# A transformer stack with routed experts on one core: the experts' entry ordered by token tile, and weight splits moved around the last branch

## The reference, cut to what matters

```python
# merged = sum over branches of sigmoid(gate) * (branch @ w_br)
x = x + merged @ w_o                       # [256, 1024] @ [1024, 1024]
h = rmsnorm_2(x, g_ffn)
g_logits = h @ w_rg + b_rg                 # 4 groups
p_g = softmax(g_logits); g_sel = argmax(g_logits)
e_in = (h @ w_re + b_re) of the chosen group         # 8 experts
top_v, top_i = top_k(e_in, 2)
w2 = softmax(top_v) * p_g[g_sel]
for n in range(32):                        # expert n: group n // 8
    a, b = split(h @ w_up[n])              # [1024, 512]
    out += combine[:, n] * ((silu(a) * b) @ w_down[n])   # [256, 1024]
x = x + out
```

## Time and profile before

| | |
|---|---|
| median of 3 runs | 1603.18 us |
| profiled execution | 1604.8 us, of which the span from first to last instruction is 1603.0 us |
| PE busy | 1554.6 us, 97% of the span |
| DVE busy | 1241.9 us, 77% |
| ACT busy | 865.4 us, 54% |
| mean granted TensorE clock | 0.993 of full |
| chain that ended last | PE 87%, DVE 7%, ACT 4%, DMA 1% |

### The profile page before, as it was taken

The page is one execution under the profiler, slowest core; times in us unless marked ns, Lnnn a source line. Parts: engine busy times, 40 slices in busy tenths (PEclk is TensorE's granted clock), DMA queues, the critical chain, the costliest instruction groups (busy, mean ns, idle before and its releaser), DMA issues.

```text
span 1603.0 us, 19574 instructions
## 1 busy us (share of the span) xinstructions
PE 1554.6 (97%) x7617; PEld 1264.4 (79%) x7617; DVE 1241.9 (77%) x1864; ACT 865.4 (54%) x1264; POOL 66.2 (4%) x102
## 2 busy tenths in 40 slices
PE   7999999999999999999999999999999999999997
PEld 4888886888887888868888888777788877777875
DVE  2898877988869888673596655769878779898996
ACT  3535445544345443457454544555566458686874
POOL 1110100000001000000001000000001000000000
PEclk9999999999999999999999999999999999999999
DMA  9999855988857988323376554445324459898993
GB/s 345 375 379 347 290 193 192 336 300 300 296 184 253 311 299 289 127 77 106 106 257 193 169 165 158 133 150 192 106 80 128 158 185 361 319 345 300 368 343 115
DMA packets 196339, 373.78 MB, mean 233 GB/s; under 512 B 8986, under 2 KB 102608, under 8 KB 196240
## 3 DMA queue, kind: packets, MB, share of 16 engines
q1 hardware_dynamic: 176976, 301.60, 55.2%
q0 software_dynamic: 18864, 69.76, 12.9%
q10 hardware_dynamic: 400, 1.10, 0.2%
HBM read 371.38 MB, written 1.05 MB: 232 GB/s over the span
## 4 chain that ended last, share of the span: by engine, by line
PE 87%; DVE 7%; ACT 4%; DMA 1%; issue 1%; SPq 0%; DVEq 0%; ACTq 0%
PE banks L521 24%; PE banks L523 24%; PE banks L522 24%; DVE ul L458 1%; PE banks L1571 1%; PE banks L1544 1%; PE banks L1052 1%; PE banks L632 1%; PE banks L2657 1%; ACT uh L447 1%; PE banks L2101 1%; PE banks L1558 1%; DMA raw<-in_ffn_w_in 1%; DVE full L986 1%; PE banks L585 1%
## 5 line engine op out<-in xcount | busy, mean ns | idle before, releaser
L447 ACT ACTIVATE uh<-raw 128x1024 fp32r<-128x1024 f32 (+2 forms) x548 | 570.1, 1049 | 415.1 <-PE banks L523 411.6
L458 DVE TENSOR_TENSOR ul<-raw,uh 128x1024 fp32r<-128x1024 f32 (+2 forms) x548 | 658.4, 1210 | 167.8 <-ACT uh L447 159.9
L521 PE MATMUL banks<-uh,hh 128*128 128x512 f32 (+2 forms) x1296 | 516.1, 398 | 9.8 <-DVE hl L992 6.1
L523 PE MATMUL banks<-uh,hl 128*128 128x512 f32 (+2 forms) x1296 | 503.7, 389 | 0.0
L522 PE MATMUL banks<-ul,hh 128*128 128x512 f32 (+2 forms) x1296 | 502.7, 388 | 0.0
L521 PEld LDWEIGHTS banks<-uh,hh 128*128 128x128 f32 x1296 | 244.8, 189 | 65.4 <-DVE hl L992 9.5
L523 PEld LDWEIGHTS banks<-uh,hl 128*128 128x128 f32 x1296 | 244.1, 188 | 50.6
L522 PEld LDWEIGHTS banks<-ul,hh 128*128 128x128 f32 x1296 | 245.1, 189 | 46.1 <-issue 0.5
L521 PE MATMUL banks<-uh,bh 128*128 128x512 f32 x512 | 207.5, 405 | 2.0 <-DVE bl L2830 1.8
L523 PE MATMUL banks<-uh,bl 128*128 128x512 f32 x512 | 200.1, 391 | 0.0
L522 PE MATMUL banks<-ul,bh 128*128 128x512 f32 x512 | 199.7, 390 | 0.0
(11 more groups left out here) (350 smaller groups left out, 1292.3 us busy)
## 6 DMA issues: line engine op xcount, KB each, us to landing
raw<-in_ffn_w_in SPq DMA_DIRECT2D x176, 512.0 KB, 6.5
raw<-in_w_up SPq DMA_DIRECT2D x64, 1024.0 KB, 6.4
arena<-in_ada_w POOLq DMA_DIRECT2D x60, 1024.0 KB, 6.0
raw<-in_ffn_w_out SPq DMA_DIRECT2D x44, 1024.0 KB, 5.6
raw<-in_w_down SPq DMA_DIRECT2D x32, 1024.0 KB, 6.1
raw<-in_w_in SPq DMA_DIRECT2D x22, 1024.0 KB, 5.1
raw<-in_ada_w SPq DMA_DIRECT2D x12, 1024.0 KB, 10.8
raw<-in_w_mem_kv SPq DMA_DIRECT2D x4, 1024.0 KB, 5.3
```

The lines of the kernel that those rows point to most:

```text
L447: act.e.activation(uh[r][:, 0:w], raw[m % NRAW][:, h * w:(h + 1) * w], AF.Copy).then_inc(act_done, ta.put("hi", u))
L458: dve.e.tensor_tensor(ul[r][:, 0:w], raw[m % NRAW][:, h * w:(h + 1) * w], uh[r][:, 0:w].bitcast(F32), ALU.subtract).then_inc(dve_done, tv. ...
L521: pe.e.matmul(o, a, wh, start=k + j == s0, stop=False)
L523: mm = pe.e.matmul(o, b, wh, start=False, stop=k + j == s1)
```

## The change

Five things change, all from the last branch on.

1. **Splits around the last branch.** ACT splits the last two `w_br` units of branch 1 ahead of the sigmoids of that branch (before, behind them). DVE splits one unit of `wo` ahead of its merge of c=0, and the second behind it (before, both ahead).
2. **wo by tile at its end, and the entry by tile.** The last two of the 8 `wo` units are first used for tile 0, then for tile 1. The first tile's addition to `x`, its transposes and its router product start while PE still multiplies tile 1. All three `keep_busy` blocks are changed: 10, 10 and 10 become 0, 5 and 3. ACT loads the table of the square root before the sums of squares. DVE's scaled copies of `x` (`normed`, `gx`) move behind the group's choice, and the gather takes all of tile 0 before tile 1, so that the second copy is due only halfway.
3. **Second selection.** `sel` of group 1 and the two MAX instructions are made before the gathered tokens are split, and side work no longer makes it.
4. **First experts.** ACT computes the second weight (Exp) and loads the Silu table between its splits, and the number of units that ACT and DVE split ahead in the experts 0 to 3 is capped until the middle of the expert (`FIRST_HIGH`, `FIRST_LOW`). The next group's side work starts at expert 4 of a group instead of 2.
5. **The end.** The last `md` is computed by column half, so the first half's split may start while PE is at the second. The stores of tile 1 are issued by ACT, those of tile 0 by SP.

```diff
-        def units_dve(dve, key, K, mid=None, mid_k=None):
-            k = 0
+        def units_dve(dve, key, K, mid=None, mid_k=None, ahead=None):
+            k, cap = 0, len(units) if ahead is None else dve.unit_at + ahead
             while k < K:
-                split_low(dve, dve.unit_at + NUNIT - 1)
+                split_low(dve, min(cap, dve.unit_at + NUNIT - 1))
                 u, kk, n = take_unit(dve, key)
                 if mid is not None and k >= (K // 2 if mid_k is None else mid_k):
                     mid()
-                    mid = None
-                split_low(dve, u + NUNIT - 1)
+                    mid, cap = None, len(units)
+                split_low(dve, min(cap, u + NUNIT - 1))
...
+            got = [take_unit(pe, ("wo",)) for _ in range(2)]
+            for t in range(T):
+                for i, (u, kk, n) in enumerate(got):
+                    if (t, i) == (1, 1):
+                        hf_turn_pe(pe, 0)
+                    mm = tile_products(pe, u, kk, n, KD - 2 + i, t, lh, ll, parts_ready(pe, "ga"), WO_BANKS[t], -1,
+                                       KD - 1)
...
+            split_high(act, act.unit_at + 3)
             sigmoid_act(act, 1)
             held_act(act, ("br",), 4, 2)
...
-            held_dve(dve, ("br",), 4, 2)
+            held_dve(dve, ("br",), 4, 1)
             merge_dve(dve, 1, 0)
+            split_low(dve, dve.unit_at + 1)
             plain_dve(dve, "ga", KD, hh, hl, bk=GA_BANKS, groups=(0, 1))
...
         def route_pe(pe):
-            keep_busy(pe, 7, 10)
...
-            keep_busy(pe, 0, 10)
+            keep_busy(pe, 0, 5)
...
-            keep_busy(pe, 0, 10)
-            gather_pe(pe, 0, 0, 4)
-            gather_pe(pe, 0, 1, 5)
+            keep_busy(pe, 0, 3)
+
+            pe.wait_ge(dve_done, tv("sel", 0, 1))
+            for t in range(T):
+                pe.wait_ge(dve_done, tv("gx", t))
+                for q in range(2):
...
         def route_act(act):
+            act.e.activation(st[:, 258:259], sum4[:, 0:1], AF.Sqrt).then_inc(act_done, ta.put())
...
+        def second_weight_act(act):
+
+            yield from idle(0.3)
+            yield 0.3
             act.wait_ge(dve_done, tv("dv"))
             act.e.activation(ez, dv, AF.Exp).then_inc(act_done, ta.put("ez"))
+            silu_table_act(act)
...
+        FIRST_HIGH, FIRST_LOW = {0: 7, 1: 4, 2: 4, 3: 4}, {0: 5, 1: 3, 2: 3, 3: 3}
...
+            def last_outp():
+
+                got = [take_unit(pe, ("md", 31)) for _ in range(2)]
+                for c in range(2):
+                    for k, (u, kk, n) in enumerate(got):
...
-                if b % 8 == 2 and g < 3:
+                if b % 8 == 4 and g < 3:
                     pe.later.add(next_group_pe(pe, g + 1))
...
+            store(act, 1)
...
-            for h in range(2):
-                for t in range(T):
-                    sp.wait_ge(dve_done, tv("xo", 3, t, h))
-                    sp.e.dma_start(out_ap[0, t * P:(t + 1) * P, h * 512:(h + 1) * 512],
-                                   xo[:, t, h * 512:(h + 1) * 512]).then_inc(loaded("out"), 16)
+            store(sp, 0)
```

More of the change, by code:

```diff
@@ L2524, in route_pe @@
             pe.frees(3, dve_done, tv, "flag")
-            keep_busy(pe, 0, 10)
-            gather_pe(pe, 0, 0, 4)
-            gather_pe(pe, 0, 1, 5)
+            keep_busy(pe, 0, 3)
+            pe.wait_ge(dve_done, tv("sel", 0, 1))
+            for t in range(T):
+                pe.wait_ge(dve_done, tv("gx", t))
+                for q in range(2):
+                    b = 4 + q
+                    if t == 0:
+                        pe.take(b)
+                    for k in range(4):
+                        mm = pe.e.matmul(PB[b][:, k * P:(k + 1) * P], gx[:, t, (4 * q + k) * P:(4 * q + k + 1) * P],
+                                         sel[0][:, t, :], start=(t == 0 and k == 0), stop=(t == 1 and k == 3))
+                    if t == 1:
+                        mm.then_inc(pe_done, tp.put("gather", 0, q))
+                        pe.frees(b, dve_done, tv, "low", 0, q)
         def route_act(act):
+            act.e.activation(st[:, 258:259], sum4[:, 0:1], AF.Sqrt).then_inc(act_done, ta.put())
             for t in range(T):
@@ L2754, in spread @@
                 pe.frees(6, dve_done, tv, "uel", b)
+            def last_outp():
+                got = [take_unit(pe, ("md", 31)) for _ in range(2)]
+                for c in range(2):
+                    for k, (u, kk, n) in enumerate(got):
+                        mm = tile_products(pe, u, kk, n, k, 0, lambda k, t: gT_h[1][:, k, 0:P],
+                                           lambda k, t: gT_l[1][:, k, 0:P],
+                                           lambda k, t: pe.wait_ge(dve_done, tv("uel", 31)), [2, 3], -1, 1, cols=(c,))
+                        if c == 1:
+                            mm.then_inc(pe_done, tp.put("used", u))
+                        elif k == 1:
+                            mm.then_inc(pe_done, tp.put("last", 0))
+                    pe.frees(2 + c, dve_done, tv, "y", 3, c)
+                tp.same("last", 1)
+                tp.same("down", 31)
             def outp(b):
@@ L2807, in experts_act @@
                     act.later.flush()
-                if b % 8 == 2 and g < 3:
+                if b % 8 == 4 and g < 3:
                     act.later.add(next_group_act(act, g + 1))
-                units_act(act, ("mu", b), KD, mid=(lambda: spread(b - 1)) if b else None)
+                if b == 0:
+                    act.later.add(second_weight_act(act))
+                units_act(act, ("mu", b), KD, mid=(lambda: spread(b - 1)) if b else None, ahead=FIRST_HIGH.get(b))
+                if b == 0:
+                    act.later.flush()
                 act.wait_ge(pe_done, tp("up", b))
@@ L2899, in too_many, with store @@
             return eng.e.value_load(flag[0:1, 0:1], min_val=0, max_val=1) == 1
+        def store(eng, t):
+            for h in range(2):
+                eng.wait_ge(dve_done, tv("xo", 3, t, h))
+                eng.e.dma_start(out_ap[0, t * P:(t + 1) * P, h * 512:(h + 1) * 512],
+                                xo[:, t, h * 512:(h + 1) * 512]).then_inc(loaded("out"), 16)
         def tensor(e):
```

126 lines of the change are left out of this document (70 added, 56 removed).

## The result

The changed kernel takes 1589.96 us (median of 4 runs, 1589.11 to 1593.09), the kernel before 1603.16 (4 runs, 1602.53 to 1603.52). The ratio is 0.9915, with a 95% interval of 0.9903 to 0.9927: 13.2 us less, where 10.7 were forecast (1592.5), inside the forecast's own range of 1589.5 to 1595.5 and 0.5 us above its lower end. The profiled execution took 1589.31 us.

A forecast was written before the change was run, and what follows sets the result against it. PE, busy 97% of the span, was taken as the bound. A 4.2 + B 2.9 + C 2.5 + D 1.8 = 11.4 us off the profiled 1604.8; less 0.7, 1603.2 - 10.7 = 1592.5 us, range 1589.5 to 1595.5.

The forecast's parts named there:

- Part A: Last branch: earlier splits and merge remove PE waits of 2.24 and 0.4 us and a 1.6 us clock loss; 4.2 us.
- Part B: Entry, last `wo` matmuls to first expert: tile order, later copies and fewer fillers start the experts sooner; 2.9 us.
- I take one such fall somewhere on the path: Entry: one clock fall to 1.2 GHz, costing 1.4 us after slack, lowers the gain from 4.3 to 2.9 us.
- Rival (1): Entry: thin work brings two or more further 1.2 GHz stretches, each 1.7 us, giving 1596; chance 0.14.
- Part C: First experts: PE's waits of 1.3, 0.9 and 0.3 us go; 2.5 us.
- the side work's move: Later groups, expert 2 to 4: same instructions beside the same matmuls, so 0 us.
- Part D: The end: column halves of the last `md` give 0.85 us, stores on two queues 0.95; 1.8 us.
- The 0.95 for the stores: The end: SP's 1.78 us third issue made the fourth 1.25 late; two queues avoid it, less 0.3 to 0.4.
- (2): Experts' start stays bound by ACT and DVE: C falls to 0.5, B's sums slip 1.5 us, giving 1596; chance 0.11.
- (3): Experts' loop: DVE becomes the bound, PE waits 0.4 us in each of 31, 12.4 in all, giving 1605; chance 0.03.
- (4): Changed places: removed waits return one place on, merge to `wo`'s first units, entry to gather; 1601 to 1604; chance 0.05.
- The 0.7 us taken off the median's gain: Clock fall at 1244 us, worth 1.6 us, may be in the profiled execution alone; gain cut from 11.4 to 10.7.

The follow-up runs named there:

- the last run: The kernel before with 9 filler matmuls in PE's 2.24 us wait at the turn of `ga`'s first half, nothing else; 1603.0 us, ratio 0.9997.
- the last branch alone: The kernel before with only ACT's splits moved ahead of the sigmoids and one `wo` split behind DVE's merge; 1600.05 us, ratio 0.9972.

## Why the prediction was right, and where its sizes were off

**Part A (4.2, measured 4.8).** The mechanism came as written. The clock's 1.6 was right in the profile. The stall's 2.64 was 3.16: the idle time of a wait is counted from the modelled end of the matmul before it, whose record lasts 0.39 us where the next one could start after 0.23. So each listed wait of PE costs some 0.16 more than it says, 0.3 for the two; 0.2 stays unexplained.

**Part B (2.9, measured 4.3).** The times that the forecast worked out were right to 0.2 us at `oh`, `sel`, gather and first expert. The term that was mis-sized is the one that came after it, "I take one such fall somewhere on the path". None came, in nine profiles of nine. The run without fillers and the one with the products in a row show how near it was: 3.6 and 4.8 us. Rival (1) was a true mechanism, kept off by eight fillers and by transposes between thin products. Of the 4.3 about 1.0 is the fall of before that went (23.8 against 22.85). The other 3.35 belong to the rest of part B together, the order by tile, the later copies and the 22 fillers less. No run separates them; without any fall, in the last run, the gather started 0.5 us after `sel` was ready, held up by the last ten fillers, so some of it is theirs.

**Part C (2.5, measured 3.6).** All three waits went, which were 2.5 as listed and, at 0.16 more each, 3.0. The last 0.6 isn't accounted for. That the caps, the Exp and the table load did most of it is shown by the run without them (3.1 back). What the forecast missed is that the side work's move, priced at 0, belongs to it: 1.7 us gained in the first group, 0.5 lost in the two others.

**Part D (1.8, measured 1.0).** The 0.85 for the column halves was right (0.8 to 0.9 by the run without them). The 0.95 for the stores was wrong: it took all of the 1.78 us of the third issue for time on the path, and the wait for the four ended 6.67 us after the first addition before and 6.58 after. The old end took 14.8, 14.9 and 14.4 us in its three profiles, so the 1.0 is known to some 0.3.

**Rivals.** (2) did not happen: DVE has the scale ahead of the product and no wait of PE is left in the experts 1 to 7 but one of 0.5 us at the next group's gather, which was there before. (3) did not, by a window in the experts after:

```profile
1317.00:1357.00 40.00, 40.00 (x187) 32.48 (x186) 36.94 (x38) 31.68 (x39) 0.00 (x0) 1.00 0.97 347
```

PE is never idle, and DVE has 3 us to spare. (4) is refuted by the last branch alone, where no wait came back.

**The sum.** 13.3 us by marks against 11.4: A +0.6, B +1.4, C +1.1, the moved side work -0.4, D -0.8. The 0.7 us taken off the median's gain for a fall that might be in the profiled execution alone is neither confirmed nor refuted; without it the forecast would have been 1.8 us off instead of 2.5. That the total came so near owes something to luck: three parts were set too low and the fourth too high.

## What to carry to other kernels

Before removing fillers, ask of each whether it shortens nothing and still holds the clock: here eight of them, in 2.5 us of waits, were worth 3.6 us in the trace, while 22 others could go with the new order. Spread thin matmuls between dense ones. Read a profile's gain by marks, so that what differs between two executions upstream of the change is not booked to it, and price a long DMA issue only after looking whether the transfer behind it ends later.

## What the hardware showed that was not expected

- Identical code up to U took 1202.4 to 1207.2 us in different executions; the stretches at 1.2 GHz ahead of it added up to 10.2 to 20.5 us.
- The clock, once low, stayed so into a gather that ran without a gap: without the fillers it came back 5.6 us after the gather's start, with the products in a row 3.9 us after it. In the one the gather took 6.53 us, in the other 5.59, where it took 3.84.
- The four last stores, 1 MB, took 6.3 to 6.9 us from the first addition to the end of the wait for them in all 14 profiles; with an issue of 1.78 us among them it was 6.67, with none over 0.4 us 6.4 to 6.6.
- 13.7 us at 1.2 GHz came with PE busy all the time, from 32 passes of 36 columns in a row on; Behind the 72 column products there were 3.4 us of it or more in every profile but the one with fillers between them.
